# A two-layer hybrid encoder trunk: the norm factor of each row applied behind the matrix products

## What is computed

```python
def rms_norm(x, g):
    return x * rsqrt(mean(x * x, -1) + 1e-6) * g

for l in range(2):
    h = rms_norm(x, g_mix[l])
    qa, ka, va, qb, kb, vb, qc, kc, vc, qd, kd, vd, fd = split(h @ w_in[l])
    # four attention groups; q and k of B, C and D are RMS-normalised per head
    ...
    x = x + concat(groups) @ w_out[l]
    h2 = rms_norm(x, g_ffn[l])
    if l == 0:
        x = x + (silu(h2 @ w_gate) * (h2 @ w_up)) @ w_down       # inner width 2816
    else:
        logits = h2 @ w_router                                   # 8 experts
        top_val, top_idx = top_k(logits, 2)
        gates = scatter(softmax(top_val), top_idx)
        x = x + sum(gates[:, e] * swiglu(h2, expert e) for e in range(8))   # inner width 3584
```

## Time and profile before

| | |
|---|---|
| median of 3 runs | 1490.09 us (1488.44 to 1490.50) |
| the profiled execution, its time | 1489.56 us |
| its span in the profile | 1487.7 us |
| TensorE busy | 1461.1 us (98% of the span) |
| VectorE, ScalarE, GpSimd busy | 1089.6, 907.2, 69.1 us |
| DMA | 435.24 MB, 293 GB/s on the mean |

### The profile page before, as it was taken

How to read it: one execution, slowest core, us unless ns; L and a number is a source line. 1 busy time by engine, 2 the same in 40 slices (tenths; PEclk the granted TensorE clock), 3 DMA queues, 4 the chain that set the end, 5 groups by cost and what they waited for, 6 DMA issues and landing times.

```text
span 1487.7 us, 16556 instructions
## 1 busy us (share of the span) xinstructions
PE 1461.1 (98%) x6511; PEld 1137.7 (76%) x6511; DVE 1089.6 (73%) x1253; ACT 907.2 (61%) x1206; POOL 69.1 (5%) x102
## 2 busy tenths in 40 slices
PE   7999999999999899999999999999999999999998
PEld 4665788885666678888888888888888888888886
DVE  2355535542344598998998998999899899889896
ACT  2334434431343487777777777777777777677773
POOL 1030000001020000000000000000000000000000
PEclk9999999999999899999999999999999999999999
DMA  8801555528021499999999999999999999999992
GB/s 316 303 17 57 182 189 200 194 89 349 18 97 57 171 392 393 361 379 384 367 373 385 355 366 394 369 368 378 378 359 378 384 366 370 387 357 364 396 375 87
DMA packets 180691, 435.24 MB, mean 293 GB/s; under 512 B 5568, under 2 KB 10368, under 8 KB 180480
## 3 DMA queue, kind: packets, MB, share of 16 engines
q1 hardware_dynamic: 177552, 423.11, 77.0%
q0 software_dynamic: 3056, 11.02, 1.9%
HBM read 428.33 MB, written 5.78 MB: 292 GB/s over the span
## 4 chain that ended last, share of the span: by engine, by line
PE 95%; DVE 3%; issue 1%; ACT 0%; SPq 0%; DMA 0%; ACTq 0%; DVEq 0%
PE ps L1007 13%; PE ps L1009 13%; PE ps L1008 13%; PE ps L641 10%; PE ps L895 8%; PE ps L897 8%; PE ps L896 8%; PE ps L765 4%; PE ps L872 3%; PE ps L873 3%; PE ps L871 3%; DVE unit_rounded L1775 2%; PE ps L880 2%; PE ps L715 1%; PE ps L737 1%
## 5 line engine op out<-in xcount | busy, mean ns | idle before, releaser
L1775 DVE TENSOR_TENSOR unit_rounded<-wmem,unit_rounded 128x1024 fp32r<-128x1024 f32 (+1 forms) x744 | 854.6, 1211 | 81.9 <-ACT unit_rounded L1271 81.5
L1271 ACT ACTIVATE unit_rounded<-wmem 128x1024 fp32r<-128x1024 f32 (+1 forms) x744 | 719.7, 1043 | 123.3 <-PE ps L1009 63.0
L895 PE MATMUL ps<-unit_rounded,vbuf_rounded 128*128 128x512 f32 x528 | 208.9, 396 | 1.4 <-DVE stage_rounded L1786 1.4
L897 PE MATMUL ps<-unit_rounded,stage_rounded 128*128 128x512 f32 x528 | 208.8, 395 | 0.0
L896 PE MATMUL ps<-unit_rounded,vbuf_rounded 128*128 128x512 f32 x528 | 208.7, 395 | 0.0
L1007 PE MATMUL ps<-unit_rounded,qkT_rounded 128*128 128x512 f32 x448 | 180.0, 402 | 0.0
L1007 PE MATMUL ps<-unit_rounded,hT_rounded 128*128 128x512 f32 x448 | 177.2, 395 | 0.0
L1009 PE MATMUL ps<-unit_rounded,qkT_rounded 128*128 128x512 f32 x448 | 177.0, 395 | 0.0
L1008 PE MATMUL ps<-unit_rounded,qkT_rounded 128*128 128x512 f32 x448 | 176.9, 395 | 0.0
L1009 PE MATMUL ps<-unit_rounded,hT_rounded 128*128 128x512 f32 x448 | 174.6, 390 | 0.0
L1008 PE MATMUL ps<-unit_rounded,hT_rounded 128*128 128x512 f32 x448 | 174.5, 390 | 0.0
(11 more groups left out here) (215 smaller groups left out, 1329.3 us busy)
## 6 DMA issues: line engine op xcount, KB each, us to landing
wmem<-in_w_exp_gate_dram SPq DMA_DIRECT2D x56, 2048.0 KB, 9.1
wmem<-in_w_exp_up_dram SPq DMA_DIRECT2D x56, 2048.0 KB, 9.3
wmem<-in_w_exp_down_dram SPq DMA_DIRECT2D x56, 2048.0 KB, 9.4
wmem<-in_w_in_dram SPq DMA_DIRECT2D x4, 3072.0 KB, 17.7
wmem<-in_w_ff_gate_dram SPq DMA_DIRECT2D x5, 2048.0 KB, 9.0
wmem<-in_w_ff_up_dram SPq DMA_DIRECT2D x5, 2048.0 KB, 8.0
wmem<-in_w_ff_down_dram SPq DMA_DIRECT2D x5, 2048.0 KB, 8.8
wmem<-in_w_out_dram SPq DMA_DIRECT2D x4, 2048.0 KB, 19.5
```

The lines of the kernel that those rows point to most:

```text
L895: pe.matmul(o, hhb, hi[:, b, c], start=(first and b == 0), stop=False, skip_group_check=True)
L897: mm = pe.matmul(o, hlb, hi[:, b, c], start=False, stop=(b == blocks - 1), skip_group_check=True)
L1271: act.activation(quarter_r(HIGH[l][0 if last else kind], q, cols), quarter(SETS[l][i][kind], q, cols), ACT.Copy).then_inc(hi_ready[kind], 1)
L1775: dve.tensor_tensor(quarter_r(u, q, cols), quarter(u, q, cols), quarter_r(HIGH[l][0 if last else kind], q, cols), ALU.subtract).then_inc(l ...
```

## The change

The rows x go to TensorE as they are. `norm` transposes `x` and no longer waits for `xs_ready`: at entry it waits for the load of x, elsewhere for the addition that completes x. The factor, now kept in a tile `rx[:, 2*l + (0 or 1), t]` of its own for each of the four norms, is applied where the products leave PSUM: in the squares, q/k scaling and value copies of attention, and in the SiLU and the product by it of the dense feed-forward. Of the eight multiplications that made `xs` (L1485) six go; two are kept (`router_rows`) for the rows that the experts gather. The squares of ScalarE are moved behind its reads of the transposed parts or between them. The difference of the two largest logits is multiplied by the factor behind the router's counts.

Four places are laid out anew:

- Entry: SyncE's queue has x tile 0, identity and the first gain rows, then the first part of `w_in` of D, then x tile 1 and the rest; the other gain rows follow and are transposed behind the second projection; the first half projection waits for part 0 of the transposes only.
- The last rows of the attention list: `norm(l, "y", (0, 1))` is ahead of the last two output projections, and in layer 1 the router's logits of tile 0 stand between these two. The router's counts are held in PSUM bank 0 in place of banks 2 and 3.
- The last dense step: the transposes of hidden tile 1 stand in the middle of `down` of tile 0, and the transposes of x tile 0 for layer 1 in the middle of `down` of tile 1.
- High and low of the first expert's up weights are made within `attention(1)`, where layer 0 makes its own, no longer in the router.

```diff
+            load_x(0)
             sp.dma_start(con[:, 0:P], consts[:, 0:P]).then_inc(s_id, 16)
-
-            sp.dma_start(grow[G_MIX:G_FFN, :], g_mix.rearrange("l (k c) -> (l k) c", c=P)).then_inc(s_gain, 16)
+            sp.dma_start(grow[G_MIX:G_FFN, :], g_mix.rearrange("l (k c) -> (l k) c", c=P)).then_inc(s_gmix, 16)
+            load_w_in_d(0, 0)
+            load_x(1)
+            load_w_in_d(0, 1)
+            load_w_in_d(0, 2)
...
             def norm(l, name, parts=range(4)):
                 for i in parts:
-                    t = i // 2
-                    if i % 2 == 0:
-
-                        pe.wait_ge(xs_ready, 2 * (2 * l + (name == "y")) + t + 1)
+                    t, half = i // 2, i % 2
+                    if name == "x" and l == 0:
+                        pe.wait_ge(s_x[t], 16)
+                    elif name == "x":
+                        pe.wait_ge(x_added, i + 1)
+                    elif t == 0:
+                        pe.wait_ge(pr_free[half], (l + 1) * (NPF // 2))
+                    else:
+                        pe.wait_ge(sc_free, (l + 1) * NSU)
...
                 out_project(l, 1, "A", 1)
+                norm(l, "y", (0, 1))
                 out_project(l, 1, "B", 0)
+                if l:
+                    logits(0)
                 out_project(l, 1, "B", 1)
-                norm(l, "y", (0, 1))
-                emptied(pe, l, ("y", 0))
-                emptied(pe, l, ("y", 1))
+                if l == 0:
+                    emptied(pe, l, ("y", 0))
+                    emptied(pe, l, ("y", 1))
...
                     gate_up(l, i, step, 1, src, 1, cols, 1)
+                    if l == 0 and s == n - 1:
+                        down(l, i, step, 0, 0, cols, step * 2 + 1, 1, part_of=(0, 1))
+                        transposes(1, cols, step * 2 + 2, 1)
+                        down(l, i, step, 0, 0, cols, step * 2 + 1, 1, part_of=(2, 3))
+                        down(l, i, step, 1, 1, cols, step * 2 + 2, 1, part_of=(0, 1))
+                        norm(1, "x", (0, 1))
+                        down(l, i, step, 1, 1, cols, step * 2 + 2, 1, part_of=(2, 3))
+                        return
...
-                act.activation(sq[:, 0:cols], pbank(m)[:, 0:cols], ACT.Square).then_inc(sq_ready, 1)
+                if g == "D":
+                    act.wait_ge(rx_ready, NT * 2 * l + u + 1)
+                act.activation(sq[:, 0:cols], pbank(m)[:, 0:cols], ACT.Square, scale=rx[:, 2 * l, u:u + 1]).then_inc(sq_ready, 1)
...
-                if l == 0:
-                    first_high(l, 1)
+                first_high(l, 1)
...
-                    silu(0, step * 2 + 1, 1, cols)
+                    act.wait_ge(rx_ready, NT * (2 * l + 2))
+                    silu(0, step * 2 + 1, 1, cols, rx[:, 2 * l + 1, 0:1])
...
                 if g == "B":
...
                 else:
-                    dve.tensor_tensor(stage[:, u, :].rearrange("p (h c) -> p h c", c=HD),
-                                      pbank(m)[:, :].rearrange("p (h c) -> p h c", c=HD),
-                                      spread(rq[:, u, :], 8, HD), ALU.mult).then_inc(pr_free[m % 2], 1)
+                    scaled(stage[:, u, :].rearrange("p (h c) -> p h c", c=HD), pbank(m)[:, :].rearrange("p (h c) -> p h c", c=HD),
+                           0, 8).then_inc(pr_free[m % 2], 1)
...
-                if l == 0:
-                    low(0, 0, 1, 0)
+                low(l, 0, 1, l * DENSE_STEPS)
...
             def router():
 
                 largest_two(0)
-                norm_scale(1, "y", 1)
+                add_out(1, 1)
                 number(0)
                 norm_read(1, "y", (2,))
-                low(1, 0, 1, DENSE_STEPS)
+                router_rows(1)
                 largest_two(1)
-                done(dve.tensor_tensor(dm[:], m2[:], m1[:], ALU.subtract))
-                assert routed[0] == R_DIFF
                 number(1)
```

More of the change, by code:

```diff
@@ L569, in _ @@
                 sp.wait_ge(done, 2 * (DENSE_STEPS - 1))
-            load_w_in_d(1)
+            for part in range(3):
+                load_w_in_d(1, part)
             load_w_in(1, "B")
@@ L637, in project @@
                 for half in halves:
+                    if half and m < NT:
+                        emptied(pe, l, ("x", 2 * m + 1))
                     if half and u == 0 and g == "D":
@@ L770, in out_project, with logits @@
                     mm.then_inc(sc_full, 1)
+            def logits(t):
+                if t == 0:
+                    pe.wait_ge(s_wr, 16)
+                    emptied(pe, 1, ("y", 0))
+                    emptied(pe, 1, ("y", 1))
+                for k in range(KD):
+                    mm = pe.matmul(ps[:, t, 0:E], hT[:, k, t * P:(t + 1) * P], wr[:, k, :], start=(k == 0), stop=(k == KD - 1))
+                mm.then_inc(r_pe, 1)
             def attention(l):
-                norm(l, "x", (0, 1))
+                if l == 0:
+                    norm(l, "x", (0, 1))
                 project(l, "D", 0, (0,))
@@ L1534, in scale_unit, with scaled @@
                 dve.wait_ge(rq_ready, n + 1)
+                scale = rx[:, 2 * l, u:u + 1]
+                def scaled(dst, src, heads, count):
+                    return dve.scalar_tensor_tensor(out=dst, in0=src, scalar=scale, in1=spread(rq[:, u, heads:heads + count], count, HD),
+                                                    op0=ALU.mult, op1=ALU.mult)
                 if g == "B":
@@ L1791, in one @@
                     cols = hidden_cols(s, l == 0)
[L1792 removed]
+                    hidden_scaled(l, 0, step * 2 + 1, cols)
                     low(l, i, 2, step, cols)
```

156 lines of the change are left out of this document (79 added, 77 removed).

## The result

The changed kernel takes 1476.39 us (median of 4 runs, 1475.29 to 1476.57); the kernel before, on the same chip, 1489.66 us (median of 4, 1488.44 to 1490.50). The ratio is 0.991, with a 95% interval of 0.9893 to 0.9927: 13.3 us faster, where 15.2 were forecast. The profiled execution has a span of 1474.6 us, 13.1 less than before.

A forecast was written before the change was run, and what follows sets the result against it. TensorE's own line of work was taken to bound the kernel, so only closing its holes counts. Gains of 3.3 + 4.7 + 3.1 + 4.1 = 15.2 us gave a forecast of 1474.9 us, range 1471.0 to 1479.5.

The forecast's parts named there:

- Entry: Kernel start: first projection begins at about 7.1 us, gaining 3.3 us, bounds 2.5 and 3.8.
- They land at 7.3 if 5.2 us holds: Kernel start: D's first weights, now behind three issues, land at 7.3 us if issue to landing again takes 5.2.
- The eight slow passes: First projection: eight passes kept at half speed, 6.32 us; up to 2.9 us more saved if the clock returns at once.
- Layer 0's feed-forward: Second norm of layer 0: hole closed, 3.0 us, and clock kept up, 1.6 to 1.7; sum 4.7, bounds 3.0 and 4.9.
- Dense end: Last dense step into layer 1: projection starts 2.9 us earlier, its passes save 0.2; sum 3.1, bounds 1.4 and 3.2.
- Router: Layer 1's router: second mask at 500.6, first expert product at 506.0 against 510.15; gain 4.1 us, bounds 2.0 and 5.5.
- Costed at nothing: Factor on PSUM reads, ScalarE's scale from a tile, extra waits, later load of second expert weights: 0 us.
- (a): Router and feed-forward: half the gain comes back, router 2, feed-forward 3; total gain 11.4 us, 1478.7; chance 0.14.
- (b): Entry and router: clock returns early and stays up; total gain 19.1 us, 1471.0; chance 0.14.
- (c): Expert stage: paced by its loads, router gain and 2.8 us lost; total gain 8.3 us, 1481.8; chance 0.06.
- (d): Dense stage: VectorE's product of SiLU and up dearer; slower, 1499 at 2 us each; chance 0.02.
- (e): TensorE's stretches: bound by other engines, so each hole reappears behind; no change, 1490 us; chance 0.02.

The follow-up runs named there:

- e4: Changed kernel with tile 0's second-norm transposes and the router's first logits back behind the last two output projections, both layers: 1486.13 us, ratio 0.9979.
- e1: Changed kernel with x tile 1 and the rest of D's weights issued only once D's first weights have landed: 1476.08 us, ratio 0.9908.
- e2: Changed kernel with D's first weights issued right after x tile 0, ahead of identity and gain rows: 1476.29 us, ratio 0.991.
- e9: e3's kernel with identity and mixer gain rows issued by ScalarE's queue, so D's first weights are SyncE's second issue: 1473.05 us, ratio 0.9889.
- e11: e9's kernel with one zero product in place of two ahead of the first projection: 1472.41 us, ratio 0.9885.
- e3: Changed kernel plus unread products on zeros, two ahead of the first transpose and two ahead of the first projection: 1473.63 us, ratio 0.9894.
- e6: Changed kernel with the last dense step in its old order, x tile 0's transposes behind both down products: 1478.32 us, ratio 0.9922.
- e7: Changed kernel with high and low of the first expert's up weights made in the router again: 1477.59 us, ratio 0.9917.
- e8: Changed kernel with the factor left out of the squares and q/k scaling of groups B, C and D: 1476.38 us, ratio 0.9909.
- e10: e3's kernel unchanged, timed again on the same chip as e9: 1473.73 us, ratio 0.9893.
- e5: Kernel before, factor still in front, with only the second norm's tile 0 transposes moved ahead of the last two output projections, both layers: 1492.13 us, ratio 1.0021.

## Why the prediction was right, and where it was not

**The bound and the places** were right. TensorE's line sets the time, and the gain lies in four places: 1.35, 4.86, 3.14 and 5.06 us. The prediction also named three signs of being wrong, and the trace has all three, two of them small: the first projection waits for a load at 8.96 us, beyond the 8 named; TensorE waits 0.20 us in the attention of layer 1; and the expert stage takes 977.95 us in place of 977.5. The total held since the first is worth 2 us and was met in part by the router.

**Entry: 3.3 forecast, 1.35 measured, and outside its bounds of 2.5 to 3.8.** The step that failed is "They land at 7.3 if 5.2 us holds", with the estimate of 6.5 by bytes. They landed 6.7 us after the issue, at 8.8. (Before, ten issues stood ahead of them and not nine, since the first row of that list is two.) The 5.2 us of the earlier trace rows had been read off a load that met idle DMA engines: in the kernel before, the window of 5 to 6 us, right behind its issue, shows 39 GB/s and that of 7 to 8 us 354. The estimate by bytes took the 418 GB/s of one full microsecond. In the changed kernel the windows of 1 us from 2 to 9 show 319, 256, 170, 334, 381, 401 and 356 GB/s, with x tile 0 in the first of them. In seven kernels with this order of loads it took 6.0 to 7.0 us, never 5.2, so that the step fails in all of them; but 6.7 is one draw, and where the weights landed at 6.0 and the eight passes took 5.43 (e4) the entry gained 3.02 us, within the bounds. Without the traffic behind it (e1) it took 6.8 us, and as second issue (e2, e9, e11) 6.0 to 6.2. Why a load of this size takes 5.2 us in one place and 6.0 to 7.0 in another stays open; why the rate dips to 170 from 4 to 5 us was not tried. The 0.6 us to signal of the other estimate is shown by no run. The activations were as forecast, 6.78 in "6.7 to 7.4".

**The eight slow passes** stayed slow, as I kept them: 6.38 us against 6.32. e3 shows that they are slow for want of work ahead of them. The changed kernel, e4, e6, e7 and e8 have one and the same entry, and their eight passes took 6.38, 5.43, 6.36, 5.39 and 6.72 us. The rule of the Trainium skill that I weighed there ("TensorE: Matmul & The Clock Gate", Part 1, What's actually happening: the amount that runs slow differs between runs) agrees with these traces, with a spread of 1.3 us, though they are single runs of five kernels and not five runs of one. The upper end that I gave it, an entry gain of 6.2 us, was reached by none: 1.35 to 3.02 us to the ninth pass in these five, 3.9 to 5.2 with the zeros (e3, e9, e10, e11).

**Layer 0's feed-forward: 4.7 forecast, 4.86 measured.** Both parts are seen: no hole, and 24 passes in 5.79 us where 5.6 were forecast. e4 shows what it was, the order, since the factor alone brings nothing. e5 shows that TensorE's order brings nothing either while VectorE's addition stays where it was. How much the two orders would bring without the factor is only estimated, 0.9 to 2.4 us.

**Dense end: 3.1 forecast, 3.14 measured.** The projection starts right behind the last product, as worked out. In e6, with the old order, 0.9 us of it remain, and they are the first half projection that waits for one copy in place of both ("Only this copy gates now, ScalarE's does not", said of the entry). In the changed kernel both copies fit under the passes, as worked out.

**Router: 4.1 forecast, 5.06 measured, within its bounds.** The steps to the second mask gained 504.71 - 491.55 = 13.16, less the 8.44 already there at the start of the stretch 4.72, where I had 4.1. This is the mis-sized term, and it is the same within 0.1 us in eight other traces of this router (e1, e2, e3, e6, e8 to e11). It is a sum of small ones: ScalarE's square of tile 1 ran beside the transposes and not behind them, the logits of tile 0 took 1.70 us in place of 1.92, the two additions 1.29 in place of 1.38. Behind the mask 5.10 us in place of "5.44 us, now the same" are luck: the other eight traces have 5.37 to 5.50, and gains of 4.58 to 4.78 for the whole. In windows of 4 us the granted clock is below 1.00 in only one, the second here:

```profile
488.00:492.00 4.00, 2.90 (x26) 2.71 (x25) 1.72 (x9) 0.00 (x0) 0.61 (x2) 1.00 1.03 348
492.00:496.00 4.00, 3.26 (x18) 3.19 (x17) 1.00 (x6) 1.21 (x5) 0.00 (x0) 0.57 1.03 409
496.00:500.00 4.00, 3.62 (x17) 2.80 (x16) 3.36 (x15) 1.28 (x5) 0.00 (x0) 1.00 0.75 290
```

Before, the five windows from 492 to 512 show 0.70, 0.50, 0.93, 0.50 and 0.67. VectorE freed of its 4.62 us is 2.1 of this term (e7).

**Costed at nothing: 0.9 us were lost.** 0.48 in attention 0, most of it the transpose of the other gain rows, which was moved in among the projections and which I did not count. 0.43 in attention 1: TensorE waits 0.20 us for VectorE's reads with the factor at B's transposes (442.22), and e8 shows the loss gone to 0.16 without the factor; but it is 0.08 with the factor in e3, where VectorE gets `rq` 0.36 us sooner. "If each were 0.1 us dearer that is 4 us spread over 300 us in which TensorE is what others wait for" had the price right (0.09) and the cover almost: 0.1 to 0.4 us of it came through. The 0.4 us in the expert stage are not to be told from chance: its code is the same in all thirteen traces, and they spread over 1.7 us; the trace shows no wait in it that was not there before. The Trainium skill ("ScalarE: Activation LUTs") puts, in the section What ACT_TABLE_LOAD costs, an operand of one value per partition at about 93 ns on ScalarE; the 598 and 688 ns, 90 apart, agree.

**The rivals.** (a), half comes back, and (b), all of it at once, did not happen as such; the entry fell short like the one and the router exceeded like the other. (c), the expert stage paced by loads: it grew by 0.4, not by several us, and less than it varies. (d), the dearer SiLU product, and (e), holes that reappear: no trace of either. The total, 13.1 to 13.3, is at the low end of the 13 to 17 that I called my forecast, since the errors of 2.0 at entry, 0.9 in what was costed at nothing and 0.4 in the expert stage were met by 1.2 elsewhere, 0.3 to 0.5 of it the router's luck.

## What to carry to other kernels

Moving a per-row factor behind a matrix product does not by itself shorten anything: with the old order it gave back 0.4 us at one norm and nothing at the other (e4), since the products ahead of the transposes already covered it. First look whether the tensor engine waits for the scaled rows at all. It pays because the transposes can then be issued ahead of the last products, and the products fill the wait, if the other engines' queues are put in the same order (e5). Ask also what a wait names: a half product that needs one copy should not wait for both, which was worth 0.9 us in e6. At a kernel's start ask of each load when it lands, not when it is issued; and fill TensorE's wait for the first loads with products on zeros, which was worth 2.8 us here, but with no more of them than fit into the wait (e9 against e11).

## What the runs showed that I had not expected

- A 1 MB load landed 5.2 us after its issue when it was issued at 4.9 us, and 6.0 to 7.0 us after it when it was issued at 2.1, in seven kernels with the same loads in the same order. A difference below 1 us between two single traces says nothing about it.
- At the start of the expert stage, too, traces of the same code differ: up to 0.8 us between e9 and e10, by when the granted clock comes back from 0.50.
- At the same entry, in five kernels, the eight first passes took between 5.39 and 6.72 us, and 5.41 and 6.32 at the other entry (e5 and the kernel before). Two kernels that differ elsewhere can differ by 1.3 us from this alone, and the granted clock of the windows there reads 1.00 all the while; only the spacing of the passes shows it.
- Products on zeros kept the passes behind them at full speed: four of them, between 1.45 and 8.22 us in TensorE's waits for the first loads, brought the transposes from 1.97 to 1.12 us and the eight passes from 6.38 to 3.67 (e3).
- A factor per partition costs VectorE 0.06 us on a read of 128x512 from PSUM (692 to 751 ns).
